# Gates of 384 tokens written by adding indirect DMAs instead of one-hot matmuls, with the low parts of the up weights on VectorE

## The reference

```
q = (h @ w_query).reshape(T, 8, 2, 128)
s1, s2 = scores of q against 2 x 128 sub-keys
v1, i1 = top_k(s1, 16);  v2, i2 = top_k(s2, 16)
top_s, top_pos = top_k(v1[:, None] + v2[None, :], 16)      # of 256 candidates
expert_idx = i1 * 128 + i2 at top_pos
gates = softmax(top_s)
y[t] = sum over 8 heads, 16 picks: gate * gelu(expert_u[idx] . h[t]) * expert_v[idx]
```

## Time and profile before

| what | value |
|---|---|
| time, median of 3 runs | 1440.53 us (1440.34 to 1441.02) |
| time of the profiled execution | 1441.41 us |
| its span, first to last instruction | 1439.4 us |
| granted TensorE clock | 1.000 |
| PE busy | 1431.6 us (99%) |
| DVE busy | 1133.4 us (79%) |
| POOL busy | 979.8 us (68%) |
| ACT busy | 574.4 us (40%) |
| DMA | 381.57 MB, mean 265 GB/s |

### The profile page before, as it was taken

The page is one execution under the profiler, slowest core; times in us unless marked ns, Lnnn a source line. Parts: engine busy times, 40 slices in busy tenths (PEclk is TensorE's granted clock), DMA queues, the critical chain, the costliest instruction groups (busy, mean ns, idle before and its releaser), DMA issues.

```text
span 1439.4 us, 20447 instructions
## 1 busy us (share of the span) xinstructions
PE 1431.6 (99%) x7551; PEld 1277.2 (89%) x7551; DVE 1133.4 (79%) x1876; ACT 574.4 (40%) x799; POOL 979.8 (68%) x533
## 2 busy tenths in 40 slices
PE   9999999999999999999999999999999999999998
PEld 7766798899999999999999999888888888888887
DVE  6678551769999999699999995498777777777775
ACT  5775453333333333444444444333333333333332
POOL 3421544346888788866766675599887888878883
PEclk9999999999999999999999999999999999999999
DMA  6221332235778888989999986998888888888883
GB/s 227 103 89 45 103 113 100 89 100 184 251 262 268 273 272 273 348 281 364 355 360 355 372 296 230 371 383 340 346 346 346 327 326 345 344 341 328 331 302 117
DMA packets 122293, 381.57 MB, mean 265 GB/s; under 512 B 11768, under 2 KB 28280, under 8 KB 122240
## 3 DMA queue, kind: packets, MB, share of 16 engines
q1 hardware_dynamic: 70384, 202.69, 39.5%
q0 software_dynamic: 36864, 134.23, 25.3%
q10 hardware_dynamic: 14992, 44.06, 7.8%
HBM read 336.89 MB, written 44.06 MB: 265 GB/s over the span
## 4 chain that ended last, share of the span: by engine, by line
PE 95%; DVE 2%; DMA 1%; ACT 1%; issue 0%; SPq 0%; DVEq 0%
PE bank L748 28%; PE bank L749 28%; PE bank L750 28%; PE bank L1004 6%; PE bank L936 1%; DMA wf<-a_dram 1%; PE bank L884 1%; PE bank L907 0%; PE wide L896 0%; DVE pad L1235 0%; PE bank L815 0%; PE wide L815 0%; PE bank L826 0%; PE bank L822 0%; PE wide L822 0%
## 5 line engine op out<-in xcount | busy, mean ns | idle before, releaser
L484 POOL TENSOR_TENSOR wl<-raw,wh 128x1024 fp32r<-128x1024 f32 x208 | 507.7, 2442 | 277.7 <-ACT wh L514 275.1
L748 PE MATMUL bank<-hh,wh 128*128 128x384 f32 (+1 forms) x1184 | 416.2, 352 | 0.2 <-DVE hl L1251 0.2
L749 PE MATMUL bank<-hl,wh 128*128 128x384 f32 (+1 forms) x1184 | 406.4, 343 | 0.0
L750 PE MATMUL bank<-hh,wl 128*128 128x384 f32 (+1 forms) x1184 | 406.4, 343 | 0.0
L748 PE MATMUL bank<-wh,Wh 128*128 128x512 f32 x768 | 299.0, 389 | 0.7 <-DVE Wl L1458 0.7
L750 PE MATMUL bank<-wh,Wl 128*128 128x512 f32 x768 | 298.8, 389 | 0.0
L749 PE MATMUL bank<-wl,Wh 128*128 128x512 f32 x768 | 298.8, 389 | 0.0
L514 ACT ACTIVATE wh<-raw 128x1024 fp32r<-128x1024 f32 (+1 forms) x217 | 227.8, 1050 | 141.4 <-PE bank L750 136.4
L748 PEld LDWEIGHTS bank<-hh,wh 128*128 128x128 f32 x1184 | 222.8, 188 | 7.9 <-DVE hl L1251 0.6
L749 PEld LDWEIGHTS bank<-hl,wh 128*128 128x128 f32 x1184 | 222.8, 188 | 7.1 <-issue 0.2
L750 PEld LDWEIGHTS bank<-hh,wl 128*128 128x128 f32 x1184 | 222.3, 188 | 7.6
(11 more groups left out here) (200 smaller groups left out, 1628.6 us busy)
## 6 DMA issues: line engine op xcount, KB each, us to landing
raw<-uT_dram SPq DMA_DIRECT2D x128, 512.0 KB
xraw<-v_dram SPq DMA_DIRECT2D x72, 512.0 KB, 8.5
raw<-v_dram SPq DMA_DIRECT2D x56, 512.0 KB, 9.1
a_dram<-act_a ACTq DMA_DIRECT2D x64, 384.0 KB
wf<-a_dram SPq DMA_DIRECT2D x32, 768.0 KB, 6.8
raw<-wst_dram SPq DMA_DIRECT2D x40, 512.0 KB
gates_dram<-gbuf ACTq DMA_DIRECT2D x32, 512.0 KB
gt<-gates_dram SPq DMA_DIRECT2D x32, 512.0 KB, 4.0
```

The source lines that it names most:

```text
L484: pool.tensor_tensor(wl[:, n % SPLIT, :], raw_of(n), wh[:, n % SPLIT, :].bitcast(F32), ALU.subtract).then_inc(w_lo, 1)
L748: pe.matmul(dst, ah, bh, start=start, stop=False)
L749: pe.matmul(dst, ah, bl, start=False, stop=False)
L750: return pe.matmul(dst, al, bh, start=False, stop=stop)
```

## The change

- The one-hot matmuls, their DVE and ACT steps, the stores and `gbuf` go. In their place there is one table `gates_dram` of (expert low index, chunk, token) with 6291456 float32 (25.2 MB).
- SP zeroes the table in 32 DMAs (`clear`), two behind each of the weight loads 5 to 20, from 1 KB of zeros in SBUF that is read again and again.
- DVE computes an address for each pick of the dense tokens (`spots`). POOL issues for each block and pick slot one indirect DMA (`scatter`) that adds 128 gates (4 bytes each) to the table: 3 blocks x 8 heads x 16 = 384 DMAs. Before a head's 16 it waits until all earlier scatters of that block have landed, since two heads may pick the same expert.
- The softmax is done per sender (a block and half of the heads): `center`, an exponential on ACT, `normalize`, the last in the middle of the next `retrieve`. The order of rounds is now (1,0), (0,0), (1,1), (0,1), (2,0), (2,1), (3,0), (3,1).
- POOL makes no low parts of the 124 up chunks; DVE does (`split_up`), placed by a count of elements between the retrieval steps (`SHARE`), then one after the other with the dots.
- POOL's gathers of `expert_u` follow a table (`ROWS_BESIDE`): none for the first sender, 12 in the second, 8 in each of the next three, 16 in the last, and 76 after the last scatter. Then come the low parts of the downs.
- SP loads the first gates once all scatters have landed; a quad's gates and activations are multiplied in one instruction. In the downs the rows come at 4.5 a quad instead of 4.

```diff
-    g_dram = nc.dram_tensor("gates_dram", (SENT, P, NCH, HALF), F32, kind="Internal").ap()
+    g_dram = nc.dram_tensor("gates_dram", (P, NCH, DT), F32, kind="Internal").ap()
+    g_flat = g_dram.rearrange("p c (t o) -> (p c t) o", o=1)
...
+            def clear(i):
+                size = NCH // CLEARS
+                sp.dma_start(g_dram[:, size * i:size * (i + 1), :].rearrange("p c t -> p (c t)")
+                             .rearrange("p (r e) -> p r e", e=BLANK),
+                             blank.unsqueeze(1).broadcast_to([P, size * DT // BLANK, BLANK])).then_inc(cleared, 16)
...
+            def row(j):
+                if j == 0:
+                    pool.wait_ge(picks_ready, 1)
+                if j >= PICKS + ROWS:
+                    pool.wait_ge(first_added, j - PICKS - ROWS + 1)
+                elif j >= ROWS:
+                    pool.wait_ge(dots_done, j - ROWS + 1)
...
+            def scatter(b, h):
+                for k in range(TOPK * h, TOPK * h + TOPK):
+                    pool.indirect_dma_start(out=g_flat, out_offset=bass.IndirectOffsetOnAxis(
+                                                ap=spots[:, b - 1, k:k + 1], axis=0),
+                                            in_=sel[:, 2, b, h, k % TOPK:k % TOPK + 1], in_offset=None,
+                                            compute_op=ALU.add).then_inc(scattered[b - 1], 16)
+            def send_gates():
+                rows = 0
+                pool.wait_ge(cleared, 16 * CLEARS)
+                for i, (b, hg) in enumerate(SENDERS):
+                    pool.wait_ge(spots_ready, i + 1)
+                    pool.wait_ge(sel_ready, SOFT.index((b, hg)) + 1)
+                    for h in range(4 * hg, 4 * hg + 4):
+                        if h:
+                            pool.wait_ge(scattered[b - 1], 16 * TOPK * h)
+                        scatter(b, h)
+                        for j in range(rows, rows + ROWS_BESIDE[i][h % 4]):
+                            row(j)
+                        rows += ROWS_BESIDE[i][h % 4]
+                for j in range(rows, PICKS):
+                    row(j)
...
+            def split_up():
+                nonlocal splits
+                n, splits = UP_W + splits, splits + 1
+                dve.wait_ge(w_hi, made_hi(n))
+                dve.tensor_tensor(wl[:, n % SPLIT, :], raw_of(n), wh[:, n % SPLIT, :].bitcast(F32), ALU.subtract)\
+                   .then_inc(u_lo, 1)
...
-            for g in range(GROUPS):
-                s, at = g % 2, slice(GROUP * g, GROUP * g + GROUP)
...
+            for i in range(ups_left):
+                split_up()
+                for j in range(dots + i * dots_left // ups_left, dots + (i + 1) * dots_left // ups_left):
+                    dot(j)
...
-                        for t in range(GROUP):
-                            last = pe.matmul(bank[GP + of % 2][:, t * P:(t + 1) * P], oh[:, of % 2, 1, t, :],
-                                             oh[:, of % 2, 0, t, :], start=True, stop=True)
-                        last.then_inc(oh_used, 1)
```

More of the change, by code:

```diff
@@ L47 @@
 PICKS = PH * TOPK
[L48 to L54, removed]
 QUAD = 4
@@ L152, in program @@
         mixers.close()
[L155 to L167, removed]
-        wf.insert(0, sb("wf0", [P, QUAD, DT], where=ups))
-        Wh.insert(0, sb("Wh0", [P, QUAD, DT], F32R, ups))
-        Wl.insert(0, sb("Wl0", [P, QUAD, DT], F32R, ups))
-        ups.close()
+        dense.close()
+        late = ExitStack()
+        xraw = sb("xraw", [P, VRAW - RAW, D], F32, late, "right")
+        gt = [sb(f"gt{i}", [P, QUAD, DT], F32, late, "right") for i in (1, 2)]
+        wf = [sb(f"wf{i}", [P, QUAD, DT], F32, late, "right") for i in (1, 2)]
+        Wh = [sb("Wh1", [P, QUAD, DT], F32R, late, "right")]
+        Wl = [sb("Wl1", [P, QUAD, DT], F32R, late, "right")]
         retr = ExitStack()
@@ L657, in _, with exponentials @@
             act.activation(identr[:, :], ident, ACT.Copy).then_inc(identr_ready, 1)
-            act.sem_inc(gp_used, FREE_BANKS)
+            def exponentials(u):
+                b, hg = u
+                heads = slice(0, PH) if b == 0 else slice(4 * hg, 4 * hg + 4)
+                act.wait_ge(gd_ready, SOFT.index(u) + 1)
+                act.activation(ge[:, b, heads, :], best[:, b, heads, :], ACT.Exp).then_inc(ge_ready, 1)
             def save_scores(k):
@@ new lines, in normalize @@
+            def normalize(u):
+                b, hg = u
+                heads = slice(0, PH) if b == 0 else slice(4 * hg, 4 * hg + 4)
+                n = heads.stop - heads.start
+                assert splits >= EXP_UPS.get(u, 0)
+                dve.wait_ge(ge_ready, SOFT.index(u) + 1)
+                work(n * TOPK, dve.tensor_reduce(gs[:, b, heads], ge[:, b, heads, :], AX.X, ALU.add))
+                fence()
+                work(n, dve.reciprocal(gr[:, b, heads], gs[:, b, heads]))
+                fence()
+                dve.tensor_tensor(sel[:, 2, b, heads, :], ge[:, b, heads, :],
+                                  gr[:, b, heads].unsqueeze(2).broadcast_to([P, n, TOPK]), ALU.mult)\
+                   .then_inc(sel_ready, 1)
@@ L1305, in retrieve @@
+            def retrieve(b, hg, dots, before):
                 heads = slice(4 * hg, 4 * hg + 4)
@@ L1419, in _ @@
-            dve.wait_ge(pick_gelu, 1)
-            dve.tensor_tensor(pick_a[:, :], pick_a[:, :], sel[:, 2, 0, :, :].rearrange("p h k -> p (h k)"), ALU.mult)\
-               .then_inc(pick_ready, 1)
+                    spend(D)
+            dots, before = 0, None
+            for u in UNITS:
+                n = DOTS_UNIT if u[0] > 1 else 0
+                if u == UNITS[1]:
+                    owed = -24000
+                retrieve(*u, tuple(range(dots, dots + n)), before)
+                before = None
+                dots += n
+                if u in SOFT:
+                    center(u)
+                    before = u
+                print(u, splits)
@@ new lines, in _ @@
+            assert dots == DOTS_RETR
+            for i in range(4):
+                split_up()
+                if i < 3:
+                    dot(dots + i)
+            dots += 3
+            normalize(before)
+            ups_left, dots_left = NCH - UP_EARLY - splits, PICKS - DOTS_LATE - dots
+            for i in range(ups_left):
+                split_up()
+                for j in range(dots + i * dots_left // ups_left, dots + (i + 1) * dots_left // ups_left):
+                    dot(j)
@@ L1498, in _constants @@
     c[:, C_ONES:C_ONES + P] = 1.0
+    for b in range(DB):
+        c[:, C_TOK + b] = P * b + p
     for g, w in enumerate(WINDOWS):
```

413 lines of the change are left out of this document (188 added, 225 removed).

## The result

The changed kernel takes 1977.12 us (median of 4 runs, 1976.56 to 1978.64); the kernel before, on the same chip, 1440.57 (1440.34 to 1441.02). The ratio is 1.3726, with a 95% interval of 1.3702 to 1.3749. Slower was forecast and slower it is, but the forecast was 1652 us with a range of 1450 to 1900: the time lies outside it, and the loss is 537 us instead of 211. The profiled execution took 1978.64 us with a span of 1976.5.

The account below looks back on a forecast made before the run. POOL's line of scatters and gathers was to replace PE as the bound: 85 us leave PE but 296 us of idle PE come, 211 us more than before. Downs from 1123 us plus 527 gave span 1650, time 1652 us; range 1450 to 1900.

Parts of the forecast that it names:

- POOL's line: Before the downs, 384 scatters and 128 gathered rows in one line on POOL become the bound: 512 x 1.26 = 645 us.
- 384 scatters at 1.26 us: POOL's scatters priced like an `expert_u` gather: 0.96 us plus a 0.30 us gap each.
- upper bound of 1.74: Highest period allowed for a scatter on POOL: 1.44 us, half as much work again for the add, plus 0.30.
- Rival B: Adds are bound by the DMA engines; a scatter would take 2.4 us, the kernel 2070 us; chance 0.06.
- Rival A: Scatters much cheaper than gathers, so POOL keeps up; faster below 0.69 us each, 1364 to 1375 us; chance 0.14.
- the zeroing: Clearing 25.2 MB beside weight loads 5 to 20, costed at nothing; up to some 50 us if its cover failed.
- the longer downs: The down stage was forecast to stay at 527 us; more than 530 us was a sign of being wrong.
- The rows of the tail: After the last scatter, 76 rows on POOL at 1.26 us each: 95.8 us.
- the 390 that it gave itself for full engines: DMA rate in GB/s when full, from the downs' 343 at a share of 0.88, used to cost the zeroing.
- The port: POOL's indirect DMAs issued during DVE's two-SBUF-tile subtractions or products lose 0.5 us each in the mean; no loss: 68 us less.
- Landings: POOL's waits for scatters to land, 4.0 us each (ends 2.5 and 8.0); six before the first row, 24 us.
- The first scatter: POOL's start after the first retrieval round, its softmax and small steps: forecast at 301 us.

Follow-up runs that it names:

- late rows: On the changed kernel, 120 of the 128 `expert_u` rows move behind the last scatter and DVE makes all gates before its dot products: 1994.57 us, ratio 1.3847.
- early rows: On the changed kernel, 40 of the 76 rows behind the last scatter move in between the scatters: 1930.92 us, ratio 1.3394.

## Why the prediction was wrong

**The direction and the path were right.** POOL's line bounds the kernel, DVE stands at a dot product from 423 us (it was busy until 574.73 - 151.26) where 420 was forecast, and the way from the first row's issue to the next sender was 75.4 us against 81 with landing. In the chain POOL's scatters lead.

**The step that failed is the term "384 scatters at 1.26 us", the price of the gather.** In its place stand 1.85 us (1.547 + 0.30), and 49 pauses that add 1.9 us each to the usual gap, a wait that the sum did not have at all. For 368 scatters in the line that is 368 x 0.59 = 217 us, and 94 for the pauses. The upper bound of 1.74 was exceeded too: with the pauses the average is 2.1 us. In the stretch to the first row the account closes: 112 x 0.587 = 66 us for the scatters, 28 for 15 pauses, less 10 us of landing and 13 of port that did not come, is 71 us, and 70.9 were measured. A bound "half as much again" was a guess without a row; where no row shows an operation, the range has to be wide enough for that, and here its cost with the pauses was 1.7 times the gather's.

**Rival B came nearer than the forecast, by luck.** Its 2070 us, 93 us above the measured time, come from 2.4 us a scatter at the DMA engines. But the engines' share is 0.41 to 0.50 in those stretches, and with twice the memory for descriptors half the pauses go. The share is still lower, 0.19, in the run with late rows, and the pauses are the same. Rival A fell, since a scatter takes 1.85 us and not less than 0.69, and its time fell with it: with the scatters gone it is 1416 us instead of 1364 to 1375. Of these 41 to 52 us, 7 are the zeroing, 19 PE's idle time where 76 rows come in one run, and 18 the longer downs; the prediction costed all three at nothing.

**The rows of the tail** (the 76 and the 4 ahead of them) were costed at POOL's 1.26 us a row. They cost 2.0 us each there, because they and the weights of the ups held back until then share engines that are full at 412 GB/s: 48 us. The prediction had what it takes to see it: a row of 512 KB every 1.26 us is 416 GB/s, more than the 390 that it gave itself for full engines, before a single weight is loaded.

**Terms that were too high.** The port was costed at 68 us. By the trace it is 618.7 - 384 x 1.547 = 25 us on scatters and 146.0 - 128 x 0.962 = 23 us on rows, 48 in all. The price of 0.5 us was right, the count was not: some 95 indirect DMAs (59 scatters, 36 gathers) started within a subtraction or product of DVE, 0.5 us each, where the sum has 137 of such losses. Two gathers of the changed kernel and the subtractions in which they started:

```profile
578.42 1.22 DVE L1284 TENSOR_TENSOR wl<-raw,wh 128x1024 fp32r<-128x1024 f32 x1
579.23 1.23 POOL L463 DMA_INDIRECT picked<-u_dram,picks  x1 [0.30 <-issue]
...
620.72 1.22 DVE L1284 TENSOR_TENSOR wl<-raw,wh 128x1024 fp32r<-128x1024 f32 x1
620.89 1.87 POOL L463 DMA_INDIRECT picked<-u_dram,picks  x1 [0.30 <-issue]
```

Both end 0.82 us after the subtraction, though one started late in it and the other early. All 36 gathers of `expert_u` that started within an L1284 end 0.80 to 0.92 us after it, and the 36 scatters that did end 1.41 to 1.52 us after it. Beside it the Trainium skill's page "SBUF — State Buffer", in the section on the bandwidth-pool intuition, lets a DMA blocked by a VectorE copy end about 115 ns after that instruction, which would have made the term nearly nothing; behind the subtractions here no gather and no scatter ended that soon.

Landings were costed at 4.0 us each, 24 in the first stretch; POOL waited 13.8 us in 6 such waits, and none of the 13.5 us set down for them in the next three senders came. The page "DMA: Bandwidth & Descriptors" of the Trainium skill (section "Anatomy of one DMA") gives a fixed 2.0 us for a DMA. The plain scatters of the run without the add agree, with 2.1 us from issue to landing in the median; an adding one takes 3.0 us in three runs that show it (late rows, early rows, 1024 bytes) and 3.5 in the one with half the scatters.

**Smaller terms.** The first scatter starts 13.5 us late, of which the zeroing makes 7. The downs take 19 us longer. PE waits 7.4 us for POOL's low part of the second chunk behind gathers of `expert_v`. Some 5 us more go in the first 40 us, where the granted clock is 0.76 and then 0.90. And from 1500 us on, at full clock and with PE busy all the time, the trace has 436 or 437 matmuls in 100 us where it had 443 before:

```profile
1500.00:1600.00 100.00, 100.00 (x437) 81.53 (x436) 64.07 (x47) 33.79 (x30) 83.24 (x46) 1.00 0.96 375
```

The earlier trace rows has 443 between 1000 and 1100 us, at a DMA share of 0.88 instead of 0.96. That makes 6 to 7 us over the stage; its cause stays open.

## What to carry to other kernels

In these runs an indirect DMA of 128 indices costs POOL 0.96 us plain, whether it moves 4 bytes or 4 KB per index, and 1.55 with an add, plus a gap of 0.30; with half the indices the adding one still costs 1.41. Hundreds of them in one line have to be compared with the matmuls they replace before the change is made (here 1.85 us and a share of pauses, 384 times, for 85 us of PE). And before an operation is exchanged, look whether a cheaper type of the same operation takes the time away: the one-pass one-hots gave 20 us for a change of type, where rounded gates are allowed, and DVE, the engine next in line, kept the rest.

## What was not expected of the hardware

- The add costs POOL 0.59 us an instruction, 1547 against 958 ns.
- POOL pauses about 2 us after every 7th adding scatter in a line, and after every 14th plain one, with 2048 bytes of memory for descriptors; 4096 bytes halved the pauses and took 44 us off the kernel, 1024 added 194.
- An indirect DMA that starts within one of DVE's subtractions of two SBUF tiles ends a fixed time after it: 0.80 to 0.92 us for a gather, 1.41 to 1.52 for an adding scatter.
- The time of an adding scatter depends little on its indices: 1547 ns for 128, 1411 for 64.
- In no fortieth of any run's span did the DMA engines move more than 415 GB/s; they stood at 409 to 415 for long stretches, at a share of 1.02 or 1.03.
- What stays open: what POOL waits for in a pause, why with 1024 bytes the pauses are three times as many as with 2048 and not twice, and why the matmuls of the downs came 1.4% slower.
